# Hybrid RWKV-7 and differential-attention layer on one core: turned forms copied by two engines, and the beginning in token halves

## The reference

```python
hn = rms_norm(h, pre_norm_w)            # h = meta tokens + x, 528 x 2048
proj = hn @ w_in                        # r, k, v, two low-rank inputs, gate; q, k, v, gate
y_r = rwkv7_branch(...) * silu(g_r)     # 16 heads x 64
y_d = diff_attn_branch(...) * silu(g_d) # 8 heads, two softmax maps each, values of width 128
y = concat([y_r, y_d]) @ w_out
out = (h + rms_norm(y, post_norm_w))[16:]
```

## Time and profile before

| | |
|---|---|
| median of 3 runs | 1368.49 us (1368.04 to 1368.84) |
| the profiled execution | 1368.25 us |
| its span, first to last instruction | 1366.4 us |
| mean granted TensorE clock | 0.996 |
| busy: TensorE, VectorE, ScalarE, GpSimd | 95%, 52%, 51%, 22% |

### The profile page before, as it was taken

The page is one execution under the profiler, slowest core; times in us unless marked ns, Lnnn a source line. Parts: engine busy times, 40 slices in busy tenths (PEclk is TensorE's granted clock), DMA queues, the critical chain, the costliest instruction groups (busy, mean ns, idle before and its releaser), DMA issues.

```text
span 1366.4 us, 24244 instructions
## 1 busy us (share of the span) xinstructions
PE 1299.5 (95%) x9393; PEld 1107.9 (81%) x9393; DVE 713.9 (52%) x1653; ACT 700.2 (51%) x1670; POOL 304.7 (22%) x234
## 2 busy tenths in 40 slices
PE   3999999999999999999999999999999999999996
PEld 2988788787887879788788788798888988678885
DVE  5346766867577686766866434343343433530013
ACT  4435766566665666666566534344453444442321
POOL 3340001000010100001000333334334343334443
PEclk9999999999999999999999999999999999999998
DMA  6221121111212111121112222222222222226333
GB/s 215 70 80 57 48 58 46 57 53 50 57 48 64 48 55 57 48 57 48 55 49 69 78 70 70 70 70 78 71 77 78 70 77 73 67 93 224 101 97 141
DMA packets 151265, 102.27 MB, mean 75 GB/s; under 512 B 6398, under 2 KB 140640, under 8 KB 149600
## 3 DMA queue, kind: packets, MB, share of 16 engines
q1 hardware_dynamic: 151152, 100.72, 24.7%
HBM read 96.50 MB, written 4.19 MB: 74 GB/s over the span
## 4 chain that ended last, share of the span: by engine, by line
PE 78%; DVE 8%; ACT 8%; issue 4%; POOL 1%; DMA 0%; ACTq 0%; DVEq 0%; SPq 0%
PE tile L569 45%; PE tile L835 2%; PE tile L836 2%; PE tile L837 2%; PE ma L805 2%; ACT arena L1097 2%; PE ma L680 2%; ACT w_hi L932 1%; PE mb L820 1%; PE ma L671 1%; PE ma L712 1%; PE ma L835 1%; PE ma L837 1%; PE ma L836 1%; PE mb L835 1%
## 5 line engine op out<-in xcount | busy, mean ns | idle before, releaser
L569 PE MATMUL tile<-hn_hi,w_hi 128*128 128x264 f32 (+1 forms) x1696 | 445.0, 325 | 0.0
L569 PE MATMUL tile<-hn_hi,w_lo 128*128 128x264 f32 (+1 forms) x1696 | 437.5, 321 | 0.0
L569 PE MATMUL tile<-hn_lo,w_hi 128*128 128x264 f32 (+1 forms) x1696 | 436.6, 320 | 0.0
L932 ACT CAST w_hi<-w_raw 128x512 fp32r<-128x512 f32 x324 | 200.3, 619 | 336.1 <-PE tile L569 231.6
L1243 POOL TENSOR_TENSOR w_lo<-w_raw,w_hi 128x512 fp32r<-128x512 f32 x196 | 254.9, 1302 | 443.0 <-ACT w_hi L932 442.9
L569 PEld LDWEIGHTS tile<-hn_hi,w_hi 128*128 128x128 f32 x1696 | 276.1, 189 | 27.4 <-issue 10.2
L569 PEld LDWEIGHTS tile<-hn_hi,w_lo 128*128 128x128 f32 x1696 | 275.6, 189 | 15.1 <-issue 3.4
L569 PEld LDWEIGHTS tile<-hn_lo,w_hi 128*128 128x128 f32 x1696 | 275.2, 189 | 11.1 <-issue 2.2
L1258 POOL TENSOR_TENSOR arena<-arena,power 128x10 f32<-128x10 f32 (+3 forms) x28 | 44.0, 1570 | 598.5 <-DVE arena L1427 462.4
L1097 ACT ACTIVATE arena<-ma 64x192 f16<-64x192 f32 x240 | 78.0, 325 | 43.1 <-PE ma L671 40.6
L1507 DVE TENSOR_TENSOR w_lo<-w_raw,w_hi 128x512 fp32r<-128x512 f32 x128 | 87.4, 683 | 1.3
(11 more groups left out here) (250 smaller groups left out, 2087.0 us busy)
## 6 DMA issues: line engine op xcount, KB each, us to landing
w_raw<-w_in SPq DMA_DIRECT2D x260, 256.0 KB, 2.9
w_raw<-w_out SPq DMA_DIRECT2D x64, 256.0 KB, 3.0
big<-x SPq DMA_DIRECT2D x4, 1024.0 KB, 7.9
arena<-x SPq DMA_DIRECT2D x4, 1024.0 KB, 8.6
out<-big SPq DMA_DIRECT2D x3, 1024.0 KB, 3.9
arena<-post_norm_w SPq DMA_DIRECT2D x1, 1024.0 KB, 4.9
out<-big SPq DMA_DIRECT2D x2, 512.0 KB, 3.2
arena<-table_rope SPq DMA_DIRECT2D x2, 264.0 KB, 2.8
```

What stands on the lines that cost most here:

```text
L569: last = mm(o[:, at:at + n], w[:, slot, cols], t[:, kt, tok:tok + n], start=(kt == 0 and w is w_hi and t is hn_hi), stop=(kt == KT - 1 and ...
L932: nc.scalar.copy(w_hi[:, slot, :], w_raw[:, slot, :]).then_inc(s("hi_done"), 1)
```

## The change

Six edits, together:

- **The turned form.** ScalarE copies its upper block, VectorE the lower one (`take_xt_lower`); the product waits for both and is put 0.15 of a step later.
- **Casts in order of places.** The weight casts of ScalarE and the low halves of GpSimd are generators with places (`weights_act`, 4k + 0.8; `weights_pool`, 4k + 1.6) and no longer stand at the head of each unit.
- **Centred v.** v is turned by a product with the centring matrix, so y comes out centred; the product of y with it goes, and so does ScalarE's copy of the result. The squares are taken from `ysum` itself.
- **r from its 15th column.** The r tile is projected from token 14 on (`FIRST` in place of `FULL`): 514 columns, as 250 and 264.
- **Beginning in token halves.** The meta tokens come as 128x256, x in another order among the other loads; TensorE multiplies the identity with itself 4 and 20 times (`keep_clock`) while it waits; 32 steps turn two blocks each (blocks 0 and 1 for all 16 feature blocks, then 2 and 3) into four homes, with the low-rank product in halves four steps behind. The squares of block 1 are shared between ScalarE and VectorE.
- **Attention places and output.** Attention iterations 9 to 11 get other places and iteration 10 may carry over too; the first two blocks of y are split before the end of the last projection, and the first output product begins with rows 2 and 3.

Several places (`GN_AT`, `NORM_AT`, `PADS_AT`, `BONUS_AT`) move a little.

```diff
+AHEAD_Y = 2
...
-FULL = {"rwkv": (True, True, True, False), "attn": (False, True, True, False)}
+FIRST = {"rwkv": (0, 0, META - 2, None), "attn": (None, 0, 0, None)}
...
+WARM = 20
...
-        GN_AT, GN_SPREAD, GN_TURN, GN_DVE = 18.5, 7.1, 9.5, (10.25, 12.2, 14.5)
+        GN_AT, GN_SPREAD, GN_TURN, GN_DVE = 18.5, 7.1, 9.25, (10.25, 12.2, 14.5)
...
-        PADS_AT = (46.2, 48.1, 49.2, 51.25)
...
+        PADS_AT = (46.2, 47.6, 48.9, 50.3)
...
-            return {FIRST_ATTN: 12, FIRST_ATTN + 1: 8.4}.get(i, 0)
+            return {FIRST_ATTN: 12, FIRST_ATTN + 1: 12.4, FIRST_ATTN + 2: 4.8}.get(i, 0)
...
-            start, step = {FIRST_ATTN: (21.8, 12.0), FIRST_ATTN + 1: (11.5, 12.4)}.get(i, (6.5, 13.0))
-            return start + step * qi
+            return {FIRST_ATTN: 22.4, FIRST_ATTN + 1: 14.8, FIRST_ATTN + 2: 8}.get(i, 6.5) + 13 * qi
...
-            return max(4 * k - 7, -1) if k < KT - 1 else 200
+            return 60.4 + 1.6 * k if k < AHEAD_Y else max(4 * k - 7, -1) if k < KT - 1 else 200
...
+        def turn_home(j):
+            return (ma, mb)[j // 2 % 2][:, j % 2 * 512:j % 2 * 512 + 2 * P]
+        def turned_tokens(j):
+            return j % KT, slice(META, FIRST_HALF) if j < KT else slice(FIRST_HALF, L)
...
+            sp.dma_start(xm, meta_tokens.rearrange("r (k c) -> (r k) c", c=MW)).then_inc(s("meta_in"), 16)
+            sp.dma_start(c32[:, 0:2 * P], c32_dram[:, 0:2 * P]).then_inc(s("ident_in"), 16)
+            load_x(0)
+            load_x(1)
...
+            load_lora(0)
+            load_x(2)
+            load_lora(1)
+            load_x(3)
+            for h in range(2, UPT):
+                load_lora(h)
+            sp.dma_start(c32[:, 2 * P:], c32_dram[:, 2 * P:]).then_inc(s("const_in"), 16)
...
+                parts = (((EDGE + full, full, L // 2 - full), (512, L // 2, L // 2)) if full is not None
+                         else ((0, META, SEQ),))
...
+            def keep_clock(count):
+                for _ in range(count):
+                    mm(tiles[0][:, 512:512 + P], ident, ident, start=True, stop=True)
...
+                part, k = divmod(j, KT)
+                at, tok, n = ((512 - FIRST_HALF, 0, FIRST_HALF), (512, FIRST_HALF, L - FIRST_HALF))[part]
+                h, c = divmod(k, UK)
+                cols = slice(c * P, (c + 1) * P)
+                pe.wait_ge(s("hn_lo_made"), j + 1)
+                pe.wait_ge(s("lo_done"), h + 1)
+                for n_, (w, t) in enumerate(((w_hi, hn_hi), (w_hi, hn_lo), (w_lo, hn_hi))):
+                    last = mm(tiles[0][:, at:at + n], w[:, h, cols], t[:, k, tok:tok + n],
+                              start=(k == 0 and n_ == 0), stop=(k == KT - 1 and n_ == 2))
+                if part and c == UK - 1:
+                    last.then_inc(s("unit_used"), 1)
...
+            pe.wait_ge(s("ident_in"), 16)
+            keep_clock(4)
+            pe.wait_ge(s("norm_sq"), 1)
+            mm(mb[:, 0:1], c32v("group"), norm_s[:, 4:5], start=True, stop=True).then_inc(s("meta_summed"), 1)
+            keep_clock(WARM)
+            pe.wait_ge(s("par_in"), 16 * 10)
+            nc.tensor.transpose(tiles[1][:, 512:512 + N_PAR], par_rows[0:N_PAR, :], ident[0:N_PAR, 0:N_PAR]
+                                ).then_inc(s("par_turned"), 1)
+            pe.wait_ge(s("meta_ready"), 1)
+            for m in range(2):
+                last = nc.tensor.transpose(tiles[1][:, m * P:(m + 1) * P], xm[:, m * P:(m + 1) * P], ident)
+            last.then_inc(s("meta_turned"), 1)
+            pe.wait_ge(s("par_made"), 1)
+            for j in range(2 * KT + LORA_LAG):
+                if j < 2 * KT:
+                    part, k = divmod(j, KT)
+                    if j >= 4:
+                        pe.wait_ge(s("hn_lo_made"), j - 3)
+                    for t in (2 * part, 2 * part + 1):
+                        if k in (0, KT // 2):
+                            pe.wait_ge(s(f"x_scaled{t}"), 1 if k == 0 else 2)
+                        last = nc.tensor.transpose(turn_home(j)[:, t % 2 * P:(t % 2 + 1) * P],
+                                                   xin[:, t, k * P:(k + 1) * P], ident)
+                    last.then_inc(s("x_turned"), 1)
+                if j == LORA_LAG:
+                    pe.wait_ge(s("meta_lo"), 1)
+                if j >= LORA_LAG:
+                    lora_part(j - LORA_LAG)
...
-                mm(o[:, 0:SEQ], c32v("centre"), ysum, start=True, stop=True).then_inc(s("centre_done"), 1)
-                yield gn_at(work) + 4
-                pe.wait_ge(s("centre_taken"), n * 2)
+                pe.wait_ge(s("y_squared"), n)
...
-                    yield level_at(g, l, 1)
+                    yield level_at(g, l, 1.15)
                     pe.wait_ge(s("zz_taken"), n * 5 + (l - 5))
                     if l > 1:
                         pe.wait_ge(s("xt_taken"), n * 5 + (l - 1 - 5))
+                        pe.wait_ge(s("xt_lower_taken"), n * 5 + (l - 1 - 5))
...
-                            last = nc.tensor.transpose(bank(1, c), xv[:, ch * CH:(ch + 2) * CH], ident)
+                            last = mm(bank(1, c), xv[:, ch * CH:(ch + 2) * CH], c32v("centre"), start=True, stop=True)
...
+                    if n + k + t == 0:
+                        pe.wait_ge(s("tile_freed"), N_TILES)
...
-                    pe.wait_ge(s("tile_freed"), N_TILES)
-                    for k in range(KT - 1):
+                    out_feature(0, 0, gens, rows=(2, 3, 0, 1))
+                    for k in range(1, KT - 1):
...
+            square_sum(4, 0)
+            square_sum(0, 1)
+            square_sum(1, 2, slice(0, D // 2))
+            split_hi(0, 0, 1)
+            square_sum(2, 3)
...
                   scale=par[:, PC["pre"] + k:PC["pre"] + k + 1]).then_inc(s("hn_hi_made"), 1)
-                if k < UPT:
-                    split_hi(k, k, 1)
-                elif k % UK == 2 and k >= UPT + UK:
-                    u = UPT + (k - UPT) // UK - 1
+                if j == 1:
+                    square_sum(3, 4)
+                elif j in (3, 6, 9):
+                    split_hi(j // 3, j // 3, 1)
...
-                A(t512, gn_home(work)[:, 0:SEQ], ACT.Copy).then_inc(s("centre_taken"), 1)
-                A(t512b, gn_home(work)[:, 0:SEQ], ACT.Square).then_inc(s("centre_taken"), 1)
+                A(t512b, ysum, ACT.Square).then_inc(s("y_squared"), 1)
...
                 def take_xt(l):
                     act.wait_ge(s("xt_done"), n * 5 + (l - 5))
-                    for rows in halves:
-                        last = A(g3(xt16)[rows, :, rows], g3(ma[:, 512:512 + W])[rows, :, rows], ACT.Copy)
-                    last.then_inc(s("xt_taken"), 1)
+                    A(g3(xt16)[top, :, top], g3(ma[:, 512:512 + W])[top, :, top], ACT.Copy).then_inc(s("xt_taken"), 1)
...
+            def weights_act(i):
                 for k in range(KT):
+                    yield k * UK + 0.8
+                    if i or k:
+                        split_hi(unit_of(i, k + AHEAD), (k + AHEAD) % RING, i * 4 + (2 + (k + AHEAD) // UPT))
...
+            def take_lo(j):
+                k, tokens = turned_tokens(j)
+                dve.wait_ge(s("hn_hi_made"), j + 1)
+                STT(hn_lo[:, k, tokens], turn_home(j), par[:, PC["pre"] + k:PC["pre"] + k + 1],
+                    hn_hi[:, k, tokens].bitcast(F32), ALU.mult, ALU.subtract).then_inc(s("hn_lo_made"), 1)
...
+            scaled(2, 1, 2)
+            dve.wait_ge(s("norm_sq"), 4)
+            variance(2, norm_s[:, 2:3])
...
+            for j in range(2 * KT):
+                take_lo(j)
+                if j == 3:
+                    dve.wait_ge(s("norm_sq"), 5)
+                    variance(3, norm_s[:, 3:4])
+                elif j in (6, 10):
+                    scaled(*((3, 2) if j == 6 else (4, 3)))
...
+                def take_xt_lower(l):
+                    dve.wait_ge(s("xt_done"), n * 5 + (l - 5))
+                    V.tensor_copy(g3(xt16)[bottom, :, bottom],
+                                  g3(ma[:, 512:512 + W])[bottom, :, bottom]).then_inc(s("xt_lower_taken"), 1)
...
+                    if l > 1:
+                        yield level_at(g, l, 0.55)
+                        take_xt_lower(l - 1)
```

More of the change, by code:

```diff
@@ L96, in constants @@
     causal = np.where(t <= s, 0.0, NEG).astype(np.float32)
-    f32 = np.concatenate([ident, masks, centre, block, heads, heads / HD, causal], 1).astype(np.float32)
+    group = (s // (P // META) == t // (P // META)).astype(np.float32)
+    f32 = np.concatenate([ident, group, masks, centre, block, heads, heads / HD, causal], 1).astype(np.float32)
     levels = [ident]
@@ L118 @@
 _n = 0
-for _name, _w in (("ident", P), ("masks", 2 * CH), ("centre", P), ("block", P),
+for _name, _w in (("ident", P), ("group", P), ("masks", 2 * CH), ("centre", P), ("block", P),
                   ("heads", 2), ("heads_mean", 2), ("causal", P)):
```

240 lines of the change are left out of this document (113 added, 127 removed).

## The result

| | before | after |
|---|---|---|
| median | 1368.26 us (4 runs) | 1348.92 us (4 runs, 1347.8 to 1352.1) |
| the profiled execution; its span | 1368.25; 1366.4 us | 1348.25; 1346.3 us |
| TensorE reaches iteration 0 at | 49.41 us | 40.08 us |
| a steady iteration | 82.23 us | 81.23 us |

The ratio is 0.9862 (0.985 to 0.9873): 19.3 us faster, where 40 us were forecast; the time lies 6 us above the stated range. The lines of after that answer to the earlier trace rows: the page's first part, and TensorE's waits (line, releaser, us in total, times, longest).

The account below looks back on a forecast made before the run. TensorE, busy 95% of the span, was taken as the bound, so terms were its gaps or work: 12.0 + 15.0 + 2.4 + 2.4 + 3.5 + 4.7 = 40.0 us less, 1328 us; forecast 1322 to 1335, wider range 1316 to 1343 us.

Parts of the forecast that it names:

- beginning: Before iteration 0: token halves let TensorE finish turning and low-rank projection at 37.4 instead of 49.4 us, 12.0 us less.
- lower copy and casts: Recurrence levels: the product with z no longer waits for ScalarE's copies and casts, net 15.0 us less, bounds 2 and 21.
- centred v, 514 columns: Recurrence work on TensorE: centring products go, 2.4 us less; fewer columns in the r products, another 2.4 us less.
- attention places: Attention iterations: shorter TensorE waits at lines 812 and 782, 3.5 us less, bounds 0 and 6.
- output: Output start: early splits of y remove 3.18 us of TensorE idling and 1.7 us of half clock; 4.7 us less.
- the price of the copy on VectorE: Recurrence: VectorE takes on 5 us an iteration; 1.3 us more charged for line 760's wait for the chain's copies.
- Rival 1: Recurrence: VectorE's lower copy is late as often as the upper was; 15.0 us become 2, 1341 us; chance 0.15.
- Rival 4: Recurrence: VectorE falls behind in each level and in-order TensorE waits; 1376 us; chance 0.02 for anything beyond 1366 us.
- the loss at the upper bound: Beginning: pauses at 14 and 17 us leave TensorE at 1.2 GHz, so it ends at 42.4 us, 7 less.
- the allowance of 2 us: Beginning: 2 us allowed for VectorE's scaling of two blocks and GpSimd's low halves between its powers, giving 37.4 us.

Follow-up runs that it names:

- e4: Only centred v and the 514 columns of r, put on the kernel before: 1362.1 us, ratio 0.9952.
- h1: f1 plus an unread VectorE maximum over 64x200 constants (about 0.36 us) at each lower copy's place, without a wait: 1337.6 us.
- e1: Only the lower-block copy on VectorE, with its later places, put on the kernel before: 1376.9 us, ratio 1.0063.
- f1: The changed kernel with ScalarE copying both blocks of the turned form again, all else staying changed: 1326.0 us, ratio 0.969.
- e2: Only ScalarE's casts and GpSimd's low halves in the order of places, put on the kernel before: 1352.1 us, ratio 0.988.
- g1: f1 plus, at each lower copy's place on VectorE, a wait for the turned form and an unread maximum over 64x288 constants: 1349.1 us.
- e3: The lower copy on VectorE with its later places and the casts in order of places, put on the kernel before: 1368.9 us, ratio 1.0001.
- g4: f1 without the 24 warm-up products of the identity with itself at the beginning: 1326.7 us, ratio 0.9696.
- h3: The changed kernel with the lower copy behind the level mask in VectorE's order instead of ahead of it: 1344.0 us, ratio 0.9818.
- h4: f1 plus VectorE's wait for the turned form and the unread 64x200 maximum at each lower copy's place: 1342.9 us, ratio 0.9812.
- f2: The kernel before with casts in order of places and the later places of the z product and x and v copies: 1349.6 us.

## Why the prediction was wrong, point by point

| term | forecast | measured in the traces |
|---|---|---|
| beginning | -12.0 | -9.3 |
| lower copy and casts (waits, iterations 0 to 8) | -15.0 | -5.1, with the next row as it is |
| centred v, 514 columns (work) | -4.8 | -4.8 put in as forecast, some -3 by e4's parts |
| attention places (iterations 9 to 14, less their work) | -3.5 | 0.0 |
| output (iterations 15, 16) | -4.7 | -2.6 |
| a half-clock stretch in iteration 6 | 0 | +1.6 |
| sum | -40.0 | -20.2 (the span fell by 20.1) |

The traces give iterations 0 to 8 together, 7.5 us less. With 3 us for the work the waits' row would be about -7.

**The step that failed** is the price of the copy on VectorE: "Against that VectorE takes on 15 x 0.33 = 5 us in an iteration of 82.2 us, in which it is busy for 58.25 us", and then "I charge 1.3 us more". I looked for the slack of the copy itself and found it (0.7 to 0.9 us): the product with z did get faster, from 2.84 to 1.60 us. I had named what is queued behind the copy, but priced it by a share of busy time. h1 priced it: an operation of 0.36 us on VectorE at 120 places costs 11.6 us, 27% of its own time (43 us), at an engine that is idle for a quarter of the iteration. The idle time is not there when the level work and the chain's copies come together. And the copy's own time was the wrong size for the queue: 0.33 us in the sum, 0.36 in its row, 0.63 as what stands behind it feels it.

**Rival 1** came nearest: VectorE's order is the cause, and it left 2 us of this term where 5 to 7 came; but the waits sit at the chain and the closing product, hardly at the lower copy. The beginning, the attention, the output and the half-clock stretch make up the rest, less what this term gave beyond the 2 us. **Rival 4's** mechanism, which I gave 2 in 100, is the true sign of this edit alone: e1 is slower than the kernel before. It did not decide, since each level lost 0.19 us (22.9 / 120), not the 0.33 us more from which it would.

**The casts** were under-priced by about as much. I gave them 2 us and the share of line 712 that both edits remove; alone they bring 16.3 us, and in f1 the waits of iterations 0 to 8 fall by 26 to 28 us (with 4.8 or 3 us for the work). That the forecast of 1328 us fits the kernel without the lower copy (1326.0) is luck, for the terms of the sum differ: two parts that attack the same wait were costed as one, and the one that did nothing for it was not costed alone.

**The beginning** was mis-sized by 2.7 us. The arrival of block 3 at 17.5 us where I had 16 accounts for 1.6 us. The half clock, which I had as the loss at the upper bound, lasted 10 us, and holding the clock full gave 0.3 us back, less than kernels with the same beginning differ by, so the allowance of 2 us for ScalarE and VectorE was too small.

**Centred v and r**: the centring product was worth its 0.855 us, the v products cost 0.71 us an iteration in place of 0.555, and r gave 0.18 to 0.27 us in place of 0.3 (e4). **The attention**: line 782's wait went, but the sum stayed. That the casts' new places took as much is likely from e2 (+2.7 us in iterations 9 to 11) and was not tried in the changed kernel. **The output**: the 3.2 us wait went as forecast. The 1.7 us of half clock left this place, but the profiled execution has another stretch elsewhere, so here they were no gain; 2.4 us went to line 863 behind the cast.

The Trainium skill, VectorE: DVE Perf Modes, Specifications, puts ScalarE closer to PSUM; the table of its TRN2 errata gives an estimate of 325 ns on VectorE and 303 on ScalarE for this copy. The rows agree in the order of the two and are longer: 361 ns on VectorE, 323 on ScalarE. It was still not the price of the move, which g1 shows with an operation that reads no PSUM.

## What to carry to other kernels

Work moved to an engine with more idle time is paid where that engine's own chain is dense: list what stands behind the new place until the next gap, and who waits for it, before counting the slack of the moved operation. Its row is not its price there either: compare when the next operation starts with it and without it. An edit that removes the same wait as another should be priced alone and beside the other; here the pair of experiments e2 and e3 would have stopped the copy. A wait placed in an in-order engine is free where slack follows it (0.6 us in 120) and costs where an operation and an urgent one stand behind it.

## What the hardware showed

**Half-clock stretches.** Between the beginning and the last product, most profiled executions have one to three short stretches at half clock, most of some 3.4 us, at places that change with the kernel: before at 1164.4 us, behind 3.18 us of idle TensorE, after at 538.1 us, with TensorE busy, e3 at 772 us, none in f1, g4, h1, h3 and h4. Each costs about 1.6 us. Executions of one kernel differ in them too: after took 1347.8, 1348.3, 1349.6 and 1352.1 us at mean clocks of 0.994, 0.993, 0.991 and 0.990. In after it lies in the middle of the recurrence (busy, count, clock):

```profile
538.00:542.00 4.00, 4.00 (x22) 0.57 0.19 53
```

What brings it was not tried. Of the six kernels with the old output, before, e1, e2 and e4 have their stretch within 1.3 us of the output's first product, at the wait for the split of y, but e3 and f2 have it at 772 and 761 us. So the wait at the output may well bring it there, and one execution doesn't tell whether taking the wait away takes the half clock out of the time, as I had counted.

**VectorE beside GpSimd.** The same 128x512 subtraction on VectorE took 0.69 us alone and 1.35 us when it started 0.49 us into GpSimd's 1.29 us operation, that is, 0.80 us to the end of that one and about 0.55 us more. The Trainium skill, SBUF — State Buffer, SBUF: two separate sides, says that these two share a pair of ports and that the one which comes second waits for the whole instruction of the other; the trace agrees but for 0.14 us, since waiting and 0.69 us would make 1.49.
